# A transformer block on one core: the first stage by feature tile, with seven PSUM banks open at once

## What is computed

```python
cs = silu(c)                                   # c: (1, 1024)
mod = cs @ ada_w + ada_b                       # (1, 6144), in six parts of 1024
shift1, scale1, gate1, shift2, scale2, gate2 = split(mod, 6)
h = rmsnorm(x, norm1_g) * (1 + scale1) + shift1
proj = h @ w_in                                # queries, keys, values, two gates
```

## Time and profile before

| what | value |
|---|---|
| median of three runs | 1333.67 us (1333.43 to 1338.35) |
| the profiled execution | 1333.61 us, its span 1332.3 us |
| mean granted TensorE clock | 0.985 |
| first matmul of the query/key product | 43.18 us |
| first matmul of the values | 83.54 us |
| first matmul of the heads' stage | 100.96 us |

### The profile page before, as it was taken

One profiled execution on the slowest core, in us unless ns is written; L12 is line 12 of the kernel. 1 busy time (PEld: TensorE's weight loads), 2 busy tenths in 40 slices (PEclk: granted clock), 3 DMA queues, 4 the chain that ended last, 5 costly groups with the idle time before them and its releaser, 6 DMA issues.

```text
span 1332.3 us, 23738 instructions
## 1 busy us (share of the span) xinstructions
PE 1253.9 (94%) x9926; PEld 1223.9 (92%) x9926; DVE 896.0 (67%) x1253; ACT 622.8 (47%) x955; POOL 189.8 (14%) x188
## 2 busy tenths in 40 slices
PE   1799998999999999999799999989999999999996
PEld 1798898999999999999699999989999987999996
DVE  7748878867555876655966666676665675866653
ACT  1435544666434444444544454444444455644531
POOL 4004433200122100002400001120000230000022
PEclk9999999999999999999799999989999999999998
DMA  8675556465565355565155555545556531565540
GB/s 332 236 277 184 199 203 238 160 238 211 201 200 181 127 192 186 165 202 174 42 179 167 183 172 163 178 150 179 189 190 206 174 115 60 174 190 190 188 145 32
DMA packets 66978, 238.87 MB, mean 179 GB/s; under 512 B 7286, under 2 KB 9512, under 8 KB 66872
## 3 DMA queue, kind: packets, MB, share of 16 engines
q1 hardware_dynamic: 66280, 235.17, 52.7%
q0 software_dynamic: 592, 2.19, 0.5%
HBM read 236.26 MB, written 1.07 MB: 178 GB/s over the span
## 4 chain that ended last, share of the span: by engine, by line
PE 83%; DVE 11%; ACT 2%; issue 2%; POOL 1%; DMA 0%; SPq 0%; DVEq 0%; ACTq 0%
PE G L543 26%; PE G L544 26%; PE G L545 25%; DVE sb_wlo L1274 2%; PE G L563 1%; DVE sb_sig L1297 1%; DVE sb_rstd L1318 1%; ACT sb_whi L961 1%; PE G L579 1%; PE A L618 1%; DMA sb_raw<-in_wstream 0%; DVE sb_xl L1764 0%; ACT sb_p L1237 0%; PE A L641 0%; DVE sb_X L1627 0%
## 5 line engine op out<-in xcount | busy, mean ns | idle before, releaser
L1274 DVE TENSOR_TENSOR sb_wlo<-sb_raw,sb_whi 128x1024 fp32r<-128x1024 f32 x395 | 488.2, 1269 | 95.0 <-ACT sb_whi L961 94.9
L543 PE MATMUL G<-sb_xh,sb_whi 128*128 128x256 f32 (+2 forms) x1868 | 535.4, 287 | 17.4 <-DVE sb_gu L1552 7.5
L544 PE MATMUL G<-sb_xl,sb_whi 128*128 128x256 f32 (+2 forms) x1868 | 533.3, 286 | 0.0
L545 PE MATMUL G<-sb_xh,sb_wlo 128*128 128x256 f32 (+2 forms) x1868 | 532.0, 285 | 0.0
L961 ACT ACTIVATE sb_whi<-sb_raw 128x1024 fp32r<-128x1024 f32 x395 | 404.4, 1050 | 186.1 <-PE G L545 174.3
L543 PEld LDWEIGHTS G<-sb_xh,sb_whi 128*128 128x128 f32 x1868 | 356.3, 191 | 22.4 <-DVE sb_gu L1552 8.3
L544 PEld LDWEIGHTS G<-sb_xl,sb_whi 128*128 128x128 f32 x1868 | 355.7, 190 | 0.1
L545 PEld LDWEIGHTS G<-sb_xh,sb_wlo 128*128 128x128 f32 x1868 | 355.6, 190 | 0.0
L543 PE MATMUL G<-sb_hh,sb_whi 128*128 128x256 f32 (+1 forms) x1056 | 301.1, 285 | 6.5 <-DVE sb_X L1326 4.3
L545 PE MATMUL G<-sb_hh,sb_wlo 128*128 128x256 f32 (+1 forms) x1056 | 301.5, 285 | 0.0
L544 PE MATMUL G<-sb_hl,sb_whi 128*128 128x256 f32 (+1 forms) x992 | 283.1, 285 | 0.0
(11 more groups left out here) (272 smaller groups left out, 1110.0 us busy)
## 6 DMA issues: line engine op xcount, KB each, us to landing
sb_raw<-in_wstream SPq DMA_DIRECT2D x443, 512.0 KB, 4.4
sb_bias<-bias_scratch POOLq DMA_DIRECT2D x1, 2048.0 KB, 17.0
sb_X<-in_xT SPq DMA_DIRECT2D x1, 1024.0 KB, 5.7
out_T<-sb_X SPq DMA_DIRECT2D x4, 256.0 KB, 2.2
sb_con<-in_consts SPq DMA_DIRECT2D x1, 632.0 KB, 6.9
sb_vec<-in_vecs SPq DMA_DIRECT2D x1, 82.5 KB, 2.0
sb_X<-in_metaT POOLq DMA_DIRECT2D x1, 64.0 KB, 4.8
sb_boh<-in_bias_oh SPq DMA_DIRECT2D x1, 51.0 KB
```

What stands on the lines that cost most here:

```text
L543: e.matmul(out, w_h, xs, start=k0 + s.kt == 0, stop=False)
L544: e.matmul(out, w_h, xr, start=False, stop=False)
L545: m = e.matmul(out, w_l, xs, start=False, stop=k0 + s.kt == ktotal - 1)
L1274: e.tensor_tensor(wlo[:, i % NSPLIT, 0:w], raw[:, c % NRAW, 0:w], f(whi[:, i % NSPLIT, 0:w]), ALU.subtract).then_inc(lo_done, 1)
```

## The change

The 16 chunks of `ada_w` for shift1 and scale1 are cut another way: two chunks for each feature tile kt, which hold all eight input slices of the scale and the shift of that tile. The 13 chunks of the query/key weights are ordered by kt (13 blocks for each kt), in one GEMM `qk`, and come in between: the weights of tile kt behind the scale and shift of tile kt + 2.

- `first_product` (ScalarE) forms the first product of a tile, 256 columns; `shift_scale_products` (VectorE) does the other seven, each on the result of the one before, with a wait between; `shift_scale_sum` (TensorE) sums over partitions into bank `A[0]`; `shift_scale` (VectorE) forms `g1m` and `mod` of that tile from PSUM with the bias `b1` made ahead.
- The squares of X go to ScalarE (four instructions of 512 columns), their sum to TensorE, as eight fp32 matmuls that accumulate. GpSimd now multiplies X by the reciprocal root (`y`, eight instructions, behind the small bias transfer in its queue), and ScalarE forms `tmp` and `xh`.
- TensorE does, for each kt, all 13 tiles with that kt, into seven banks (`G` and `A[1]` to `A[3]`, two tiles a bank but for the first), and they are copied out at the end, while the values `va` go into `A[0]`. The two pairs of pieces of `ada_w` part 4 lie before `va` and between `va` and `vb`.
- X is transferred behind the first two chunks, in halves; the rows of the bias come ahead of chunk 4 (before: 24), the constants ahead of `vb`; the 2 MB bias transfer is issued once the `y` are made.

```diff
-    for i in range(4):
-        for part in range(4):
-            ada(i, part)
...
+    for kt in range(KT + 2):
+        if kt < KT:
+            for half in range(2):
+                group(f"ada_h{kt}_{half}", [("ada_w", 0, _r(r * P), _r((i * KT + kt) * P)) for r in _r(4 * half, 4) for i in (1, 0)], True)
+        while kt >= 2 and done * CH < QK_TILES * (kt - 1):
+            group(f"qk_{done}", qk[done * CH:(done + 1) * CH], True)
+            done += 1
+    for part in (0, 1):
+        ada(4, part)
     group("va", [("w_in", 0, _r(kt * P), _r(o["va"])) for kt in range(KT)], True)
+    for part in (2, 3):
+        ada(4, part)
...
         def tensor_program(e):
...
+            def shift_scale_sum(kt):
+
+                e.wait_ge(acc1_done, 7 * kt + 7)
+                if kt:
+                    e.wait_ge(gain1_done, 2 * kt)
+                else:
+                    e.wait_ge(root_done, ROOT["norm1"])
+                for n in range(2):
+                    m = e.matmul(A[0][:, n:n + 1], acc1(kt)[:, n * P:(n + 1) * P], one_col[:, 0:1], start=True, stop=True)
+                m.then_inc(sum1_done, 1)
...
-            mean(0, COLS1, "x")
-            mod_sum("mod0", 0, 4)
+            for kt in range(KT):
+                if kt % 2 == 0:
+                    e.wait_ge(xsq_done, kt // 2 + 1)
+                m = e.matmul(A[0][:, 0:SEQ], mean_ones[:, 0, :], sig[:, kt, :], start=kt == 0, stop=kt == KT - 1)
+            m.then_inc(mean_done, 1)
...
+            for kt in range(KT):
+                if kt < KT - 2:
+                    shift_scale_sum(kt + 2)
                 e.wait_ge(xl_done, XSTAGE["h"] + kt + 1)
...
+                for s in steps["qk"][QK_TILES * kt:QK_TILES * (kt + 1)]:
...
+                    e.matmul(out, w_h, xh[:, kt, COLS1], start=kt == 0 and s.t in qk_first, stop=False, skip_group_check=True)
+                    e.matmul(out, w_h, xl[:, kt, COLS1], start=False, stop=False, skip_group_check=True)
+                    m = e.matmul(out, w_l, xh[:, kt, COLS1], start=False, stop=kt == KT - 1, skip_group_check=True)
...
         def scalar_program(e):
...
+            def first_product(kt):
+                c = where[f"ada_h{kt}_0"][0][0]
+                e.wait_ge(loaded[c % NRAW], 16 * (c // NRAW + 1))
+                if kt >= 2:
+                    e.wait_ge(sum1_done, kt - 1)
+                e.activation(acc1(kt), raw[:, c % NRAW, 0:2 * P], ACT.Copy, scale=csil[:, 0:1]).then_inc(first_done, 1)
+            first_product(0)
+            for n in range(4):
+                e.wait_ge((x_in, x_rest)[n // 2], 16)
+                e.activation(sig[:, 2 * n:2 * n + 2, :], X[:, 2 * n:2 * n + 2, COLS1], ACT.Square).then_inc(xsq_done, 1)
+            first_product(1)
             sqrt_mean("norm1", COLS1)
+            e.wait_ge(bias_made, 1)
+            e.activation(brows[:, :], A[1][0:HEADS1, 0:BIASC], ACT.Copy).then_inc(bias_row, 1)
             preload(ACT.Exp)
...
+            for kt in range(KT):
+                if kt < KT - 2:
+                    first_product(kt + 2)
+                split_hi(QK_NEEDED[kt])
+                e.wait_ge(y_done, kt + 1)
+                e.wait_ge(gain1_done, 2 * kt + 2)
+                if kt >= 2:
+                    e.wait_ge(xl_done, kt - 1)
+                e.activation(tmp[:, kt % 2, 0:SEQ], sig[:, KT + kt, :], ACT.Identity, bias=mod[:, kt:kt + 1], scale=g1m[:, kt:kt + 1]).then_inc(f_done, 1)
+                e.wait_ge(f_done, kt + 1)
+                e.activation(xh[:, kt, COLS1], tmp[:, kt % 2, 0:SEQ], ACT.Copy).then_inc(xh_done, 1)
...
         def vector_program(e):
...
+            def shift_scale_products(kt):
+
+                for half in range(2):
...
+                    for r in range(4 * half, 4 * half + 4):
+                        if r == 0:
+                            e.wait_ge(first_done, kt + 1)
+                            continue
+                        if r > 1:
+                            e.wait_ge(acc1_done, 7 * kt + r - 1)
+                        w = raw[:, c % NRAW, r % 4 * 2 * P:(r % 4 + 1) * 2 * P]
+                        e.scalar_tensor_tensor(acc1(kt), w, csil[:, r:r + 1], acc1(kt), ALU.mult, ALU.add).then_inc(acc1_done, 1)
+            def shift_scale(kt):
+                e.wait_ge(sum1_done, kt + 1)
+                e.tensor_scalar(g1m[:, kt:kt + 1], A[0][:, 0:1], b1[:, kt:kt + 1], V("norm1_g", kt), ALU.add, ALU.mult).then_inc(gain1_done, 1)
+                e.tensor_tensor(mod[:, kt:kt + 1], A[0][:, 1:2], V("ada_b", kt), ALU.add).then_inc(gain1_done, 1)
             e.wait_ge(silu_c, 1)
...
+            shift_scale_products(0)
+            shift_scale_products(1)
+            rstd_from("norm1", rstd, root, COLS1)
+            shift_scale(0)
+            for kt in range(KT):
+                if kt < KT - 2:
+                    shift_scale_products(kt + 2)
+                if kt < KT - 1:
+                    shift_scale(kt + 1)
+                split_lo(QK_NEEDED[kt])
+                e.wait_ge(xh_done, kt + 1)
+                e.tensor_tensor(xl[:, kt, COLS1], tmp[:, kt % 2, 0:SEQ], f(xh[:, kt, COLS1]), ALU.subtract).then_inc(xl_done, 1)
...
         def pool_program(e):
...
-            e.wait_ge(x_in, 16)
-            for kt in range(KT):
-                square(X[:, kt, COLS1], kt == 0, COLS1)
             e.wait_ge(bias_row, 1)
             e.dma_start(scratch[:, 0:BIASC], brows[:, :]).then_inc(rows_out, 16)
...
+            e.wait_ge(rstd_done, RSTD["norm1"])
+            for kt in range(KT):
+                e.tensor_tensor(sig[:, KT + kt, :], X[:, kt, COLS1], rstd[:, COLS1], ALU.mult).then_inc(y_done, 1)
             e.wait_ge(rows_out, 16)
-            e.wait_ge(left_act, plan.left_act["qk1"])
             e.dma_start(bias[:, :, :], hankel).then_inc(bias_in, 16)
```

More of the change, by code:

```diff
@@ L177, in weight_plan @@
             chunks[-1].append(b)
+    where["qk"] = [place for i in range(QK_CHUNKS) for place in where.pop(f"qk_{i}")]
     return chunks, where
@@ L254, in gemm_plan @@
 def gemm_plan():
-    out = [(f"qk{i}", 2 if i < 6 else 1, KT) for i in range(7)] + [("va", 1, KT), ("vb", 4, KT)]
+    out = [("qk", QK_TILES, KT), ("va", 1, KT), ("vb", 4, KT)]
     out += [(f"gate{i}", 2, 4) for i in range(HEADS1)] + [(f"bra{i}", 2, 4) for i in range(4)] + [(f"brb{i}", 2, 4) for i in range(4)]
@@ L265, in pair_plan @@
 def pair_plan():
-    out = [("mod0", 0, 1)] + [(f"qk{i}", 1, 1 if i < 6 else 0) for i in range(7)] + [("va", 1, 1), ("vb", 1, 1), ("mod4", 0, 1)]
+    out = [("vb", 1, 1), ("mod4", 0, 1)]
     for i in range(HEADS1 + 2):
@@ L549, in gemm, with token_major @@
                         each(s.kt)
[L551 removed]
+            def token_major(name, width, nk, src, rows, outs, ready=None, shared=False):
                 nb = width // P
@@ L562, in token_major @@
                         for j, (s_, m_) in enumerate(((xs, w_h), (xr, w_h), (xs, w_l))):
-                            t = e.matmul(outs[i][0:m, 0:width], s_, m_, start=kt == 0 and j == 0, stop=kt == nk - 1 and j == 2)
+                            t = e.matmul(outs[i][0:m, 0:width], s_, m_, start=kt == 0 and j == 0 and not (shared and i), stop=kt == nk - 1 and j == 2, skip_group_check=shared)
                     if last.closes or kt == nk - 1:
@@ new lines, in tensor_program @@
+            e.wait_ge(consts_set, 5)
+            for kt in range(KT):
[3 more added lines that the diff above has]
+            m.then_inc(mean_done, 1)
+            e.wait_ge(rows_in, 32)
+            e.matmul(A[1][0:HEADS1, 0:BIASC], brow[:, :], boh[:, :], start=True, stop=True).then_inc(bias_made, 1)
+            for kt in range(2):
+                shift_scale_sum(kt)
@@ new lines, in qk_copy @@
+            def qk_copy(i):
+                ts = QK_BANKS[i]
+                dst, ps = blocks(flat(qk[:, ts[0]:ts[-1] + 1, :])), blocks(qk_banks[i][:, 0:len(ts) * SEQ])
+                e.activation(dst, ps[:, :, :, ::-1] if 1 <= ts[0] <= 4 or ts[0] >= 9 else ps, ACT.Copy).then_inc(qk_act, 1)
+            split_hi(plan.hi_to[steps["va"][0].i])
+            e.wait_ge(mm_done, ended["qk"])
+            for i in (0, 2, 4, 6):
+                qk_copy(i)
+            splits("va")
+            e.wait_ge(mm_done, ended["va"])
@@ L1380, in vector_program @@
+            for part in (0, 1):
+                ada_piece(4, part)
+            split_lo(plan.lo_to[steps["va"][0].i])
+            e.wait_ge(mm_done, ended["qk"])
+            for i in (1, 3, 5):
+                qk_copy(i)
+            splits("va")
+            for part in (2, 3):
+                ada_piece(4, part)
+            splits("vb")
+            e.wait_ge(mm_done, ended["vb"])
+            e.tensor_copy(vtok[:, 1, P:5 * P], G[plan.pair["vb"]][:, 1, :]).then_inc(left_dve, 1)
             mod_out("mod4")
```

163 lines of the change are left out of this document (67 added, 96 removed).

## The result

| | median | range, executions | ratio to before |
|---|---|---|---|
| before | 1333.64 us | 1333.43 to 1338.35, 4 | |
| after | 1318.07 us | 1316.18 to 1321.37, 4 | 0.9869 [0.9836, 0.9902] |

The direction and the mechanism came as described, the size did not.

The account below looks back on a forecast made before the run. VectorE's 43 us with TensorE idle, then TensorE's 40.4 us, were taken to bound the stage; overlaid, the product ends at 74.1 us instead of 83.5: 1333.6 - 9.4 = 1324.2 us, range 1319.5 to 1331.

Parts of the forecast that it names:

- Behind them everything only follows, so that difference passes to the end one for one.: Work behind the values: an earlier start of the values than 83.54 us reaches the end in full, 9.4 us.
- The start: Ahead of VectorE's loop: first chunk lands at 5.7 us, loop starts at 18.5 us (17.5 to 20).
- A turn of 6.75 or 5.6 us: VectorE's loop: products 3.6 us, gain and shift 0.4, low parts 1.18 each, `xl` 0.40; 6.75 us with two chunks, 5.6 with one.
- GpSimd at +3.3 us: Turn 0 of VectorE's loop: eight GpSimd multiplies beside it each hold VectorE up once, 3.3 us in all.
- Three joined bursts: End of the query/key product: TensorE bounds from tile 5, 60.0 + 3 x 4.56 = 73.7 us, plus 0.4 for the clock.
- Rival 1: VectorE's loop: 2 MB bias transfer and weights collide, VectorE waits, at most 5.1 us lost, 1329.3 us; chance 0.12.
- Rival 2: Start and neighbours cost more: GpSimd +3.4 us, sum of squares at low clock +1.3 us, 1328.9 us; chance 0.12.
- Rival 3: Query/key product: TensorE stays at 1.2 GHz because its work comes in bursts, 9.2 us a tile, 1352 us; chance 0.08.
- Rival 4: The change does not arrive at the end: the heads take up the 9 us, for want of chunks, 1333.6 us; chance 0.06.

Follow-up runs that it names:

- the last experiment: Fastest version (two chains added, late bias transfer, nine more matmuls) with `b1` allocated behind all other tiles: 1317.87 us, ratio 0.9876.
- all shifted: Changed kernel with 32 unused bytes in front of all tiles, so that streamed and weight tiles keep their distance: 1318.13 us, ratio 0.9892.
- the doubled version: Changed kernel with GpSimd forming its eight `y` a second time, into an unused buffer: 1322.80 us, ratio 0.9924.
- two chains: Changed kernel with two accumulators for a tile, VectorE alternating between them and TensorE summing both: 1320.89 us, ratio 0.9905.
- the version with the clock up there: Changed kernel with nine more unused fp32 matmuls on TensorE ahead of the first burst, nothing else changed: 1316.72 us, ratio 0.9869.
- late-bias version: Changed kernel with the 2 MB bias transfer issued only once the last `xl` exists: 1320.15 us, ratio 0.9906.

## Why the prediction was off

**"Behind them everything only follows, so that difference passes to the end one for one."** This is the step that failed. The 12.0 us of the stage do pass: the heads start at 88.92 us for 100.96. But the matmuls behind do not keep their pace: the 32 bytes of `b1` bring those that stream `hh` and its neighbours from 120.0 to 116.7 ns, 7.7 us of TensorE's time. By three pairs that differ in the address alone this is worth 3.5, 2.8 and 3.0 to 4.1 us of the median; the first is clear of noise, the second barely, the third by its trace only. From the heads to the end of the span it took 1231.4 us before, 1231.6 in the last experiment (not shifted) and 1226.7 with all shifted, and those three executions had 30.7 us at 1.2 GHz each between 60 us and the low stretch in which all end: 4.8 us at an equal clock. Of the other 2.6 us of spacing 0.6 is the part that this run spent at 117.8 ns; where the rest goes was not tried. Without the shift the change gains 1333.45 - 1320.90 = 12.6 us, with it 15.6. The prediction has no term for `b1` and never asked where its tile lies.

**The start.** The first chunk was used at 5.0 us (5.7 forecast) and tile 0's products began at 5.69; the loop started at 18.77 us (18.5); in the traces of the experiments it starts from 17.3 us on, where the sum of squares took 5.2 us for 6.7. Right within its bounds.

**A turn of 6.75 or 5.6 us** was 6.45 or 5.3: the chain as computed (0.51 us a step, 3.59 us), but gain and shift 0.25 for 0.4, two low parts 2.27 for 2.36, `xl` 0.33 for 0.40. All three are overlaps of an instruction with the next, which a duration doesn't show; an interval between starts does. Over turns 1 to 5 that is 1.5 us.

**GpSimd at +3.3 us** was 6.00 - 3.67 = 2.3 us, 0.29 us for each `y`; the second eight of the doubled version cost 3.2 us, 0.39 us each. Shown, in the place forecast, at less than the price taken for turn 0. By the rule of the Trainium skill (GPSIMD Engine Reference, Key points) that was cited, the trace agrees.

These two terms, mis-sized by 1.5 and 1.0 us, make `xl` of tile 5 end at 57.6 us and not 60.0. **Three joined bursts** took 13.9 us for 13.7 + 0.4. The product's end was thus at 71.5 us and not 74.1: 12.0 us of gain for 9.4, inside the range with 1321.6 us, had there been nothing else.

**Rival 1, the collision**: ScalarE's waits came, VectorE had none, and moving the transfer changed nothing in the stage. VectorE waited for chunks only once it had been made faster (two chains: 3.7 us). That the transfers of all queues interleave on the same engines (the Trainium skill, Trainium Kernel Development and Optimization, Key Constraints) agrees with ScalarE's longest wait falling from 7.31 to 4.11 us when the bias goes late, and shows in nothing of the changed kernel's time. **Rival 2**: neither part came; GpSimd cost 2.3 us in turn 0 and not 6.7, and the sum of squares took 6.65 us and not 7.9. **Rival 3**: TensorE was at 1.2 GHz for the first 4 us of the product alone, and the version with the clock up there ended no earlier behind `xl` of tile 5. **Rival 4**: the heads follow the values' last sum at once, at 88.92 us.

The fastest version measured, two chains with an addition, late bias transfer and nine unused matmuls, takes 1313.78 us, 4.3 us less than the change; without the nine it is 1314.46 us. The intervals of both overlap the change's; what is shown of them is the earlier start of the values.

## What to carry to other kernels

A new tile, however small, moves every tile allocated behind it: print the addresses of the streamed operands before and after, and where a change gains or loses in stages that it doesn't touch, count the matmuls in a full window of both traces, then undo the shift alone. Where a chain of one engine sets the pace, price it by intervals between starts, not by durations, and work out at the same time how far the next engine is behind it: here shortening VectorE's products by 1.2 us a turn brought 0.8 us in all; with TensorE's sums halved again and the bias transfer late it was 2.6. An accumulation chain of 256 columns on VectorE costs 0.515 us a step where alternating two costs 0.40.

## What the runs showed of the hardware

- The interval between matmuls of 256 fp32r columns depends on where the streamed tile lies in relation to the tiles in front of it, the weights' tiles among them: 120.0 ns, 116.7 (32 bytes further), 117.7 (64 bytes further) for `hh`; 119.8, 117.0 and 115.5 for `oh`. Moving all tiles left the mean near it (117.1 for `hh`). For `xh`, 32 bytes made it 118.2 from 117.1.
- It is not fixed by the address alone: at the same addresses `hh` ran at 116.7 ns up to a stretch at 1.2 GHz and at 120.0 behind it (351 to 418 us of the late-bias version), at 117.8 in two other versions; in three traces at the old place always at 120.0.
- The granted clock after the same 26 matmul records and the same gap of 1.24 us was 1.2 GHz in one execution and 2.4 GHz in another, whose idle time in front of those records was 2.23 us for 1.71. Between 1085 and 1105 us of the changed kernel it was 1.2 GHz in the profiled execution, and 2.4 GHz at the same work in that of before. What makes it fall there is open.
- VectorE lost 0.29 to 0.39 us to each 128x256 multiply of GpSimd beside it, and ran dependent products of 256 columns 0.515 us apart where independent ones ran 0.40 us apart.
